# S5 in chunks of eight steps with powers and a block Toeplitz matrix; HGRN levels spread among the projections

## The reference

```
mod = silu(c) @ w_ada[l] + b_ada[l]                    # 1024 x 6144
z = (x * (1.0 + sc1) + sh1) @ w_in[l]                  # split: a_u a_v b_cq b_ckv b_kr c_u d_q d_f d_i d_g

# S5: 16 groups of 16 channels, 64 complex states each
abar = exp(dt * a);  bbar = (abar - 1) / a * b
h_t = abar * h_{t-1} + bbar @ u_t;   y = real(c @ h) + d * u
z = gelu(y);  y_c = z * sigmoid(z @ w_glu + b_glu)

# HGRN2: 4 heads, chunks of 64 steps
f = lb + (1 - lb) * sigmoid(f_logit);  b = cumsum(log f) within the chunk
att[t, s] = sum_k q[t,k] * (1-f)[s,k] * exp(b[t,k] - b[s,k])    # s <= t
u_chunk = ((1-f) * exp(b_last - b))^T v;  S = exp(b_last) * S + u_chunk
y_d = rms_norm(att @ v + (q * exp(b)) @ S_in) * sigmoid(g)
```

## Time and profile before

| | |
|---|---|
| time before, median of 3 runs | 1675.18 us (1673.76 to 1676.18) |
| the profiled execution, time / span | 1671.66 us / 1669.9 us |
| TensorE busy | 1502.6 us (90% of the span), 6366 instructions |
| VectorE busy | 852.4 us (51%), 1470 instructions |
| ScalarE / GpSimd busy | 538.4 us (32%) / 590.4 us (35%) |
| chain that ended last | TensorE 76%, VectorE 13%, GpSimd 4%, issue 3%, ScalarE 2% |
| DMA | 157.94 MB, 95 GB/s in the mean; 4704 packets under 512 B of 42412 |

### The profile page before, as it was taken

One profiled execution on the slowest core, in us unless ns is written; L12 is line 12 of the kernel. 1 busy time (PEld: TensorE's weight loads), 2 busy tenths in 40 slices (PEclk: granted clock), 3 DMA queues, 4 the chain that ended last, 5 costly groups with the idle time before them and its releaser, 6 DMA issues.

```text
span 1669.9 us, 16269 instructions
## 1 busy us (share of the span) xinstructions
PE 1502.6 (90%) x6366; PEld 1080.9 (65%) x6366; DVE 852.4 (51%) x1470; ACT 538.4 (32%) x785; POOL 590.4 (35%) x352
## 2 busy tenths in 40 slices
PE   5899968898999999989888996889898999998986
PEld 3353547546778888778653554763677888886865
DVE  6779567334367667633355755833435333331125
ACT  2620141035253333332235014113425333332322
POOL 0745400002664444434346440000265444443442
PEclk8898977589999999999998998757898999998997
DMA  9344300000236655545321110000021332322221
GB/s 388 127 138 152 101 13 1 1 1 28 73 130 199 199 190 191 180 162 188 116 77 49 41 64 26 1 1 0 13 89 64 101 91 99 101 89 76 95 82 50
DMA packets 42412, 157.94 MB, mean 95 GB/s; under 512 B 4704, under 2 KB 5088, under 8 KB 41824
## 3 DMA queue, kind: packets, MB, share of 16 engines
q1 hardware_dynamic: 42336, 156.91, 28.2%
HBM read 154.79 MB, written 2.10 MB: 94 GB/s over the span
## 4 chain that ended last, share of the span: by engine, by line
PE 76%; DVE 13%; POOL 4%; issue 3%; ACT 2%; DMA 1%; SPq 1%; POOLq 0%; ACTq 0%; DVEq 0%
PE bank L356 17%; PE bank L357 17%; PE bank L358 16%; PE bank L447 5%; PE bank L441 3%; PE bank L371 2%; PE bank L565 2%; PE bank L365 2%; PE bank L567 2%; PE bank L594 1%; PE bank L613 1%; DVE scr L1037 1%; PE bank L420 1%; PE bank L500 1%; DVE xa L730 1%
## 5 line engine op out<-in xcount | busy, mean ns | idle before, releaser
L1536 POOL TENSOR_TENSOR ring_r<-ring,scr_r 128x1024 fp32r<-128x1024 f32 x148 | 355.2, 2402 | 836.1 <-ACT scr_r L1271 567.9
L356 PE MATMUL bank<-ym_r,scr_r 128*128 128x512 f32 x704 | 278.0, 395 | 7.7 <-DVE hm_r L1172 7.7
L358 PE MATMUL bank<-hm_r,scr_r 128*128 128x512 f32 x704 | 278.6, 396 | 0.0
L357 PE MATMUL bank<-ym_r,ring_r 128*128 128x512 f32 x704 | 276.7, 393 | 0.0
L356 PE MATMUL bank<-scr_r 128*128 128x512 f32 x480 | 194.9, 406 | 29.4 <-issue 14.2
L357 PE MATMUL bank<-scr_r,ring_r 128*128 128x512 f32 x480 | 194.5, 405 | 0.0
L1188 DVE SCALAR_TENSOR_TENSOR scr<-bank,pb,scr 128x511 f32<-128x511 f32 x88 | 66.0, 750 | 205.6 <-ACT scr L1438 205.4
L447 PE MATMUL bank<-hm,ring 128*128 128x512 f32 x352 | 160.6, 613 | 10.5 <-ACT scr L1308 10.5
L779 DVE SCALAR_TENSOR_TENSOR ada<-ada,silu_c 128x1024 f32<-128x1024 f32 x80 | 140.6, 1764 | 49.7 <-DMA ada<-in_w_ada 49.7
L356 PEld LDWEIGHTS bank<-ym_r,scr_r 128*128 128x128 f32 x704 | 133.8, 190 | 36.1 <-issue 8.2
L357 PEld LDWEIGHTS bank<-ym_r,ring_r 128*128 128x128 f32 x704 | 133.6, 190 | 30.3
(11 more groups left out here) (290 smaller groups left out, 2134.4 us busy)
## 6 DMA issues: line engine op xcount, KB each, us to landing
ring<-in_w_up SPq DMA_DIRECT2D x88, 512.0 KB, 3.6
ada<-in_w_ada SPq DMA_DIRECT2D x80, 512.0 KB, 3.5
ring<-in_w_down SPq DMA_DIRECT2D x44, 512.0 KB, 3.5
ring<-in_w_in SPq DMA_DIRECT2D x34, 512.0 KB, 3.9
scr<-in_w_ada SPq DMA_DIRECT2D x16, 512.0 KB, 14.4
ring<-in_w_out SPq DMA_DIRECT2D x16, 512.0 KB, 3.5
pa<-in_par_a SPq DMA_DIRECT2D x2, 2144.5 KB, 14.3
xa<-in_x SPq DMA_DIRECT2D x1, 2048.0 KB, 7.9
```

The source lines that it names most:

```text
L356: first = mm(dst, w_hi, x_hi, start=start, stop=False)
L357: mm(dst, w_lo, x_hi, start=False, stop=False)
L358: return first, mm(dst, w_hi, x_lo, start=False, stop=stop)
L1536: G.tensor_tensor(ring_r[:, at, :], ring[:, at, :], wh[:, at, :].bitcast(F32), ALU.subtract)\
```

## The change

1. **Order.** The chunks of `w_in` come as F0, F1, Q0, Q1, U0, U1, I0, I1, CKV, CQ0, CQ1, G0, G1, AV0, AV1, AU0, AU1. HGRN's gate, cumulative sum and `ke` come early on VectorE and ScalarE; its transposes, state updates and levels are tasks after the projections (`between`), and the levels' operands overwrite their exponentials (`ee`). The level results are taken under the mask for the later halves alone (256 of 512 columns).
2. **S5 in chunks.** The 512 steps become 64 chunks of 8. VectorE makes abar^e bbar for e = 0..7 (`pw`) by doubling, GpSimd abar^s c for s = 1..8 (`cap`, 24 tensor_tensor). The input of S5 and `pw` go to DRAM and come back in another layout (`u_d`, `w_d`), so that a 128-row operand holds 8 steps x 16 channels. TensorE turns the powers (`s5_turn`), multiplies them with c (`s5_kernels`) to get the response at 0..7 steps, which goes through DRAM (`k_d`) to become a block Toeplitz matrix per group (`toe`); `s5_inputs` gives the state input of each chunk; one rotation, scan and back rotation of 512 columns (64 chunks x 8 tiles) follows in place of eight; `s5_outputs` adds the Toeplitz part and the part from the state. The result goes through DRAM once more (`y_d`).
3. **GLU later.** The GLU matmul, its gate and HGRN's sigmoid of G stand behind the HGRN output matmuls and the last projection. The normalization of `avt` reads `sd` behind that gate in ScalarE's order.
4. **Modulation.** The 24 tiles of layer 1 are used at other places: six before `ke`, two after level 0, three after each of the levels 1 to 4, and four after level 5 and on; on SP they follow the chunks of `MOD_AT`. The 16 early tiles share a semaphore in pairs.

The diff, cut to its core:

```diff
+WIN = [F0, F1, Q0, Q1, U0, U1, I0, I1, CKV, CQ0, CQ1, G0, G1, AV0, AV1, AU0, AU1]
+MOD_AT = {3: (0, 2), 7: (2, 6), 8: (6, 8), 13: (8, 10), 14: (10, 13), 15: (13, 16), 16: (16, 19), 17: (19, 22), 18: (22, 24)}
-    if l == 0 and 5 <= n < 5 + ST:
-        return range(3 * (n - 5), 3 * (n - 4))
+    if l == 0 and n in MOD_AT:
+        return range(*MOD_AT[n])
...
-                sp.dma_start(early[i], w_ada[0, i]).then_inc(early_in[i], 16)
+                sp.dma_start(early[i], w_ada[0, i]).then_inc(early_in[i // 2], 16)
+            def s5_traffic(l, n):
+                if n == 9:
+                    sp.wait_ge(S["s5_pow"], l + 1)
+                    for c in range(CT):
+                        sp.dma_start(w_d[8 * c:8 * c + 8].rearrange("g n e x -> (g n) e x"),
+                                     pw[:, :, c, :, :].rearrange("p e r s -> p e (r s)")).then_inc(S["s5_wd"], 16)
+                    sp.wait_ge(S["proj_out"], l * NPROJ + AT[U1] + 1)
+                    sp.dma_start(u_d.rearrange("(c p) s x -> p c (s x)", p=P), ym[:, 4:6, :]).then_inc(S["s5_ud"], 16)
+                if n == 10:
...                 # 8 loads of wvs (w_rows[e]), 8 of us (u_rows[SC - 1 - e])
+                if n == 13:
...                 # 8 stores of kd into k_d
+                if n == 14:
+                    sp.wait_ge(S["s5_v"], l + 1)
+                    sp.wait_ge(S["s5_kd"], 16 * SC * (l + 1))
+                    for e in range(SC):
+                        sp.dma_start(toe[16 * e:16 * e + 16, :, :], k_d[:, :, 16 * e:16 * e + P]).then_inc(S["s5_toe"], 16)
+                if n == 19:
...                 # 8 stores of ysp into y_d, then one load of ys
@@ TensorE
+                def s5_outputs():
+                    pe.wait_ge(S["s5_toe"], 16 * SC * (l + 1))
+                    pe.wait_ge(S["s5_h"], l + 1)
+                    pe.wait_ge(S["s5_cap"], l + 1)
+                    for t in range(ST):
+                        for hp in range(2):
+                            g = 2 * t + hp
+                            rows = slice(64 * hp, 64 * hp + 64)
+                            dst, at = banks[6 + hp], t * NSC
+                            mm(dst[:, at:at + NSC], toe[:, g, :], us[:, g, :], start=True, stop=False, skip_group_check=True)
+                            for r in range(2):
+                                last = mm(dst[:, at + 1:at + NSC], cap[rows, r, t, :, :].rearrange("p s n -> p (s n)"),
+                                          hh[rows, r, t * NSC:(t + 1) * NSC - 1], start=False, stop=(r == 1),
+                                          skip_group_check=True)
+                    last.then_inc(S["s5_ymm"], 1)
+                between = {AT[U1]: [hg_turn], AT[I0]: [], AT[I1]: [lambda: hg_update(0), lambda: s5_turn(0)],
+                           AT[CKV]: [lambda: hg_update(1), lambda: s5_turn(1)],
+                           AT[CQ0]: [lambda: level(0), lambda: level(1), s5_kernels],
+                           AT[CQ1]: [lambda: level(2), lambda: level(3), s5_inputs],
+                           AT[G0]: [lambda: level(4), lambda: level(5)],
+                           AT[G1]: [lambda: level(6), lambda: level(7)],
+                           AT[AV0]: [lambda: level(8), lambda: level(9)],
+                           AT[AV1]: [lambda: level(10), lambda: level(11), s5_outputs],
+                           AT[AU0]: [lambda: level(12), lambda: level(13)]}
@@ VectorE
+                for i, k in enumerate((1, 2, 4)):
+                    m = [d[:, 0:k * 2 * P].rearrange("p (e c r s) -> p e c r s", e=k, c=CT, r=2) for d in dm]
+                    for c in range(CT):
+                        for x in range(2):
+                            a = aps[:, i, x:x + 1, c * 64:(c + 1) * 64].unsqueeze(1).to_broadcast([P, k, 2, 64])
+                            ch.post(V.tensor_tensor(m[x][:, :, c, :, :], pw[:, 0:k, c, :, :], a, ALU.mult))
...
+                for i in range(0, 6):
+                    mods_mix(i)
                 v.wait_ge(S["hg_exp"], l + 1)
...
                 for lv in range(len(LEVELS) + 1):
...
+                    for i in range(6 if lv == 0 else 5 + 3 * lv, 8 + 3 * lv):
+                        mods_mix(i)
+                    if lv == 2:
+                        s5_in()
+                    if lv == 3:
+                        s5_out()
```

More of the change, by code:

```diff
@@ new lines, in _ @@
+                w0, w1 = chunk(l, 0), chunk(l, 1)
+                for k in range(KD):
+                    pe.wait_ge(S["h_ready"], (2 * l) * KD + (k + 1))
+                    for j, w in ((0, w0), (1, w1)):
+                        last = mm(banks[2 + j][:, :], w[:, k, :], hm[:, k, :], start=(k == 0), stop=(k == KD - 1))
+                        if k == 0 and j == 0:
+                            last.then_inc(S["chunk_used"], 1)
+                        if k == KD - 1:
+                            last.then_inc(S["proj_mm"], 1)
@@ new lines, in _ @@
+                for p in range(2, NPROJ):
+                    w = chunk(l, p)
+                    if p >= 4:
+                        pe.wait_ge(S["proj_out"], l * NPROJ + p - 1)
+                    bank = banks[p % 2]
+                    if WIN[p] in (I0, I1, AV0, AV1):
+                        for b in range(NB):
+                            for k in range(KD):
+                                last = mm(bank[:, b * P:(b + 1) * P], hm[:, k, b * P:(b + 1) * P], w[:, k, :],
+                                          start=(k == 0), stop=(k == KD - 1))
+                                if b == 0 and k == 0:
+                                    last.then_inc(S["chunk_used"], 1)
+                    else:
+                        for k in range(KD):
+                            last = mm(bank[:, :], w[:, k, :], hm[:, k, :], start=(k == 0), stop=(k == KD - 1))
+                            if k == 0:
+                                last.then_inc(S["chunk_used"], 2 if p == 2 else 1)
+                    last.then_inc(S["proj_mm"], 1)
+                    for task in between.get(p, ()):
+                        task()
@@ L815, in _ @@
-                are, aim = p_a("s5_are"), p_a("s5_aim")
-                v.wait_ge(S["s5_ang"], 3 * l + 1)
+                lg = p_a("hg_lb").rearrange("p (c j) -> p c j", j=L)
+                lb, omlb = small[:, 40:42], small[:, 42:44]
+                ch.link(V.tensor_tensor(small[:, 44:46], lg[:, :, 0], lg[:, :, 1], ALU.max))
+                for j in range(L):
+                    ins = V.tensor_tensor(small[:, 46 + 2 * j:48 + 2 * j], lg[:, :, j], small[:, 44:46], ALU.subtract)
+                ins.then_inc(S["hg_lb"], 1)
@@ L1344, in _ @@
+                for c in range(CT):
+                    A(ke[:, c, :], sg[:, c, :], ACT.Exp)
+                A(qe[:, 0, :], bc[:, 0, :], ACT.Exp)
+                A(qe[:, 1, :], bc[:, 1, :], ACT.Exp).then_inc(S["hg_exp"], 1)
+                evict(AT[U0])
+                evict(AT[U1])
                 a.wait_ge(S["hg_ktr"], l + 1)
```

721 lines of the change are left out of this document (417 added, 304 removed).

## The result

The changed kernel takes 1699.8 us in the median of four executions (1688.3 to 1708.4) against 1674.5 (1673.7 to 1676.2): the ratio is 1.0141, 95% interval 1.0101 to 1.0181. It is slower by 1.4%, where 1670 was forecast. Ten executions of it, with those of the first experiment, fall into two groups, 1688.3 to 1694.6 (four) and 1707.7 to 1722.2 (six); the kernel before has no such groups. The intervals of ratios leave out executions over 1.5% above a kernel's fastest, so for kernels with groups the medians here say more. The profiled execution took 1708.4 us (span 1706.6), 36.7 more than that of before.

What follows compares the result with a forecast made beforehand. TensorE, busy for 90% of the span, was taken as the bound. Layer 2 -7.9, layer 1 +1.5 and the start +1.3 summed to -5.1 us; forecast 1670 us, own range 1662 to 1678, eight in ten 1649 to 1692.

Steps and rivals of the forecast that it cites:

- half clock: TensorE at half speed after waits; stage A: 2.5 us in layer 2, in layer 1 another 0.9 behind three stalls.
- stage A: Mixers from first projection matmul to end of last; forecast 197.8 us against 161.0 in layer 2, 225.2 against 178.5 in layer 1.
- layer 1's stalls: TensorE held up at levels by late-loaded modulation tiles: 4.2, 4.2-like 3.9, 5.9 and 0.8, sum 14.8 us; bounds 0 and 25.
- Stage B: Mixers from last projection's end to the broadcast of HGRN's head norm; forecast 29.5 us against 74.1 in layer 2.
- TensorE's own work in stage A: Projections 121.1, level steps 24.9, HGRN turn and updates 4.6, S5 30.5; sum 181.1 us.
- The wait for `ke`: TensorE waits for VectorE before HGRN's transposes: 13.3 us in layer 2, bounds 0 to 18; GpSimd sharing costs VectorE 14.
- The third rival, the clock: Small matmuls and gaps in stage A hold TensorE's clock lower: 8 us per layer, 1686 us; chance 0.08.
- the first rival: Slower: small DMA transfers on SP cost more per issue and landing, growing layer 1's stalls; 1689 us, chance 0.22.
- the trip of the powers: Powers of B through DRAM and back, loads landing 6.4 us after issue starts, due at 9; hidden with 2.7 us cover.
- The output trip: S5's result through DRAM, two transfers in sequence: done at 11.0 us, due at 15.6; hidden with 4.6 us cover.
- The start: Early modulation tiles waited for in pairs, so VectorE's first product waits for a second tile: +1.3 us.
- Behind that point the two kernels do the same work in the same order: After the broadcast of HGRN's head norm nothing changes; no term in the sum.

Runs made afterwards that it cites:

- the first experiment: The changed kernel executed once more without any edit; median 1709.7 us, ratio 1.0169 to the kernel before.
- best1: Changed kernel with the edits of tiles2, cap_late, trip and weave, and a separate semaphore for each early modulation tile; 1607.6 us, ratio 0.9606.
- cap_late: Changed kernel with GpSimd starting the powers of C only when VectorE has finished the powers of B; 1678.8 us, ratio 1.0040.
- weave: Changed kernel with S5's small output matmuls put between the eight steps of projection AU0, not in one run behind AV1; 1684.4 us, ratio 0.9987.
- trip: On cap_late: the powers of B stored to DRAM and loaded back one weight chunk earlier; 1677.7 us, ratio 0.9977.
- tiles2: Changed kernel with layer 1's modulation tiles placed again, eight in stage A's gaps and sixteen in layer 1's attention; 1676.6 us, ratio 0.9986.
- best2: best1 with the sixteen late modulation tiles placed again around attention of layer 1; 1599.2 us, ratio 0.9551.
- before_wide: The kernel before with attention's last values matmul done thirteen times instead of once in both layers; 1708.4 us, ratio 1.0197.
- wide: Changed kernel with attention's last values matmul done thirteen times instead of once in both layers; 1736.7 us, ratio 1.0353.

## Why the prediction was wrong

The step that failed is the price of TensorE's clock. The sum has 2.5 us of half clock for stage A of layer 2, about 5 for layer 1 and nothing behind the head norm, where it says that the two kernels do the same work. The runs show 13.7 and 30.5 us in the stages, 15.6 in attention of layer 2 and 6 behind attention in layer 1. The second step is the size of layer 1's stalls, 14.8 us summed and 26.9 measured. Term by term:

**Stage B** was right and a little too dear: 26.1 and 25.5 us for 29.5. In layer 2 the output matmuls took 7.9 for 8.5, the chain from the GLU's end to the spatial matmuls 7.4 as summed (1102.26 to 1109.69), and what follows 6.5 for 6.6. The 3 us added for half clock behind the wait were not lost.

**TensorE's own work in stage A** was forecast at 181.1. At the full clock it is about 170: the 184.0 us busy in layer 2 hold 13.7 of half clock (8.0 in the outputs of S5, 2.6 and 1.5 in the projections behind small matmuls, 1.6 in the first turn). The levels run at 2.82 us for 32 instructions (0.088 each, not 0.111), S5's 288 at 25 and not 30.5. `best1` shows it in layer 2, with 168.9 busy at a clock of 0.99.

**The wait for `ke`** was right in its mechanism: 7.9 + 3.2 us in layer 2 against 13.3 + 0.9, the sharing 9.7 against 14. `cap_late` has VectorE's 16.6 us alone.

**The third rival, the clock,** was the largest miss, with a chance of 0.08. Half clock cost 13.7 us in layer 2's stage A, where 2.5 was summed, and 30.5 in layer 1's, where it was some 5. My argument against it was that the last levels of before ran at 0.111 each, the full rate. That reading was wrong: the granted clock over that row was 0.84, and the full rate is 0.088. The window of that row in the kernel before, with the columns of the earlier trace rows:

```profile
1062.63:1073.32 10.69, 10.69 (x96) 10.24 (x96) 9.23 (x16) 0.00 (x0) 0.00 (x0) 0.84 0.01 2
```

Those levels also have 128 columns, and the run of 64-column matmuls has none among them that is wider. `weave` shows the price by taking it away: 11.4 and 14.9.

**The stalls of layer 1** had the right place and cause, a third tile behind a wait, but not the right size: 26.9 us and not 14.8. The largest was 11.6 where 4.2 was worked out. VectorE and SyncE there:

```profile
173.16 5.15 SPq L377 DMA_DIRECT2D scr<-s_k  x8
178.35 9.45 SPq L344 DMA_DIRECT2D ada<-in_w_ada  x3
```

```profile
186.22 1.23 DVE L893 SCALAR_TENSOR_TENSOR ada<-ada,silu_c 128x1024 f32<-128x1024 f32 x1 [15.04 <-DMA ada<-in_w_ada]
```

The eight loads of the Toeplitz matrix took 5.15 us to issue (0.64 each, not 0.43), and the tile behind them came 7.8 us after its issue, not 3.9. It was issued right behind 1 MB in pieces of 512 bytes; that these held it up is inferred. This is the first rival's mechanism, at about its price per trip. Its other part, the trip of the powers, cost 4.3 and 4.9 us where I had a cover of 2.7; `trip` took that away. The output trip stayed hidden: TensorE never waits for it.

**The start** was right: 1.2 for 1.3.

**"Behind that point the two kernels do the same work in the same order"** is true of the instructions and false of the time. This step has no term in the sum, and it holds 18.6 of the 36.7 us of the profiled execution: attention of layer 2 runs at half clock for another 31 us in it. The 6 us in the output projection and FFN of layer 1 are the clock as well: TensorE waits as long there as before, but is busy for 435.2 us and not 429.3, at a granted clock of 0.95 and not 0.96. The executions of the lower group, 1688 to 1695, lie on both sides of the stated range's end (1692); it is the other group that puts the median outside it.

In numbers, for the profiled execution (forecast, measured): layer 1 +1.5, +25.9 (half clock +25, waits +13, work -11, stage B -3 beside the forecast); layer 2 -7.9, -8.9 (half clock +11, waits +3, work -11, stage B -4); start +1.3, +1.2; the rest 0, +18.6. That layer 2 came out as forecast is luck: its misses cancel.

What stays open: what makes the clock fall in attention in one execution and not in the next. The distance from its return to the small matmuls does not decide it: in the profiles it fell at 4.7 us (five layers), at 6.0 (layer 1 of `tiles2` and of `best1`), 6.2 (`best2`), 11.4 and 11.6, and it held at 5.9 to 6.4 in fifteen layers, at 8.4 and at 9.8. Nor does the change itself decide it (`before_wide`). The two layers of `tiles2` and `best1` had been measured before `wide` was set up, and its text leaves them out.

## What to carry to other kernels

Small matmuls are to be dealt out among wide ones, not put in a run: the same instructions cost 23 us in a run and 15 woven in. Work for a slow loader (here a third modulation tile behind another transfer) belongs into the gaps that the trace shows on the engine that uses it, issued a transfer's time ahead; the tiles' places alone made 52 us of stage A. And where two engines slow each other down, let the one whose result is due late start late: one changed wait gave 11.5 us in layer 2.

## What the runs showed of the hardware that I had not expected

- TensorE's clock falls without any gap: 3 to 5 us into a run of 64-column matmuls, and for 31 us in attention while TensorE is busy all the time (0.54 of the clock in the windows above).
- It can also stay down for long, in the kernel before too: in attention it is at 0.50 for 38 to 51 us in one piece from shortly behind the broadcast of the head norm (before 298.4 to 346.1), though TensorE waits for nothing after the first 10 us of that and works through 512-column matmuls on 96 rows for 29 us of it.
- A VectorE tensor_scalar with one input in SBUF is held up by GpSimd's tensor_tensor too: 2.33 us for two instead of 0.76. The Trainium skill, "SBUF — State Buffer", section "Who interferes with whom", lists tensor_scalar among the instructions that can take the shared port pair; the trace agrees. Had VectorE been blocked for the whole of each of GpSimd's 24 instructions, it would have lost up to 17.1 us (an estimate); 9.7 were lost.
- An issue on SyncE's queue costs 0.33 to 0.46 us for 512 KB in large pieces, 0.48 to 0.64 for the small pieces of the powers and of the Toeplitz matrix, and 0.98 for those of the input (eight in 7.84 us). The Trainium skill, "DMA: Bandwidth & Descriptors", section "Specifications", speaks of the size of a piece for the rate alone; here the issue was longer for small pieces, also for those of 512 bytes. That the size of the piece is the cause is not shown: sixteen issues of 512 KB in large pieces, one right behind the other, took 0.93 each.
